# First tokens copied ahead of the first weight split, and a reordered tail, in a one-core encoder layer

## The chip, the core and the metric

One core of a Trainium2 chip. The metric is device time in microseconds of one execution. The engines are TensorE (PE, with PEld for its weight loads), VectorE (DVE), ScalarE (ACT), GpSimd (POOL) and SyncE (SP, which here only issues DMAs and waits). Each runs its own instruction stream in order, and streams meet only at semaphores.

## The reference

Two sequences go through one layer: a sample of 1024 tokens and a prompt of 512, width 1024, float32.

```
h = rmsnorm(x, norm1_g)
proj = h @ w_in                          # q, k, v, z, xBC, dt
x = x + concat(diff_attention(q, k, v), bidirectional_ssd(z, xbc, dt)) @ w_out
h = rmsnorm(x, norm2_g)
aff = softmax(h @ w_router)              # per sequence
gate, idx = top_k(aff.T, cap)            # 16 experts, cap 128 (sample) and 64 (prompt) tokens each
ye = (silu(h[idx] @ w_gate) * (h[idx] @ w_up)) @ w_down * gate
x = x.at[idx].add(ye)
y = rmsnorm(x, final_g)
```

## The kernel before

**Precision and weights.** Every product of two float32 matrices is made of three matmuls of rounded parts: high x high, high x low, low x high. So each weight chunk of 128 x 2048 is loaded (SP), its high part is copied by ACT (`whi`, L780; in the experts L1128) and its low part is a subtraction (`wlo`): by DVE for the first chunk (L1188) and in the experts (L1749), by POOL for the chunks of the input projection (L559). Tokens are treated alike: PE turns (transposes) a normed tile (L1854), ACT copies the high part (`tokens_hi`, L796), DVE makes the low part (`tokens_lo`, L1208).

**Token tiles.** There are 12 tiles of 128 tokens, 0 to 7 of the sample and 8 to 11 of the prompt, in blocks of four: b = 0, 1 (sample) and b = 2 (prompt). A tile is loaded by POOL into one of two slots. `rms(t)` on ACT squares and sums (L786) and takes the root (L789), `normed(t)` on DVE does mean, reciprocal and scaling (L1197 to L1200).

**The opening.** DVE and ACT work out small constants. Then ACT: rms(0), rms(1), split(0); DVE: wait for the gain, normed(0), normed(1), split(0), five small set-up instructions (selectors, L1245 to L1250), and three clears (L1257 to L1259). In the block loop ACT goes tokens_hi(0), rms(2), tokens_hi(1), rms(3), tokens_hi(2), tokens_hi(3), and DVE goes tokens_lo and normed in the same order, then the sin product (L1269). PE turns tiles 0 and 1; then the first 256 token columns of column tile 0 (24 matmuls), tile 2's turn, the first 256 columns of column tile 1, tile 3's turn. It waits for all low parts and starts the steady stretch of 25 column tiles. The first matmuls need the low parts of the first chunk and of tiles 0 and 1. The three clears run at the start of each sequence, so at the prompt's too. There DVE's stretch behind the sin product holds 16 choosing rounds (`choose`, L1215 to L1217) for the sample's top-k and 8 convolution steps (L1317, L1319) beside the rotations (L1276 to L1285). POOL's splits run beside them.

**The experts.** Expert e has 12 chunks: 0 to 7 gate and up, 8 to 11 down. Chunks 8 and 9 make half 0 of the output columns, 10 and 11 half 1. At step j, ACT and DVE split chunk j + 2. Each expert's rows are scattered with an add into `acc_dram`, which holds the residual. The loop is unrolled for the last two, e = 14 (`LATE`) and e = 15.

**The tail.** The final norm needs all experts. Tiles 0 to 3 are loaded (`fin`), squared (L1095), normed (L1675) and stored while expert 14 runs, without the rows of experts 14 and 15. Tiles 4 to 11 follow during expert 15, without its rows. Rows that expert 14 changed are gathered again (`fix_s` 128 of the sample, `fix_p` 64 of the prompt), normed (L1699) and stored over the early ones by POOL (L755, L758). Rows that expert 15 changes are gathered (`xe_s`, `xe_p`), the expert's output is added on the chip half by half (`end_half`: L1720, L1721 for the prompt, L1716 for the sample), normed (L1800) and stored last by POOL (L762, L765). SP holds the stores of tiles 4 to 11 (L493) until both `fix` stores have landed; POOL holds the last two until all tiles are stored. `final_stage` says at which step of expert 14 or 15 the squares, roots and norms run, `norm_order` in which order the squares count.

Of the kernel before, what the change touches and what calls it, by code (L numbers as in the profile page):

```python
# [75 lines left out]
def hybrid_encoder(nc, x, w_in, w_out, w_moe, params, consts, rope, gains, y):  # L76
# [10 lines left out]
    with ctx:  # L87
# [91 lines left out]
        fix_s = at("fix_s", S0 + 16, [P, D])  # L179
# [32 lines left out]
        fi_s = at("fi_s", o + 3.4, [P, 1], U32)  # L212
# [70 lines left out]
        x2_out = [sem(f"x2_out{i}") for i in range(4)]  # L283
        h2_out = [sem(f"h2_out{i}") for i in range(4)]
# [12 lines left out]
        y_in = [sem(f"y_in{i}") for i in range(4)]  # L297
# [56 lines left out]
        def final_tile(t):  # L354

            if t < 11:
                return fin[:, t % 7, :]
# [65 lines left out]
        def _(sp):  # L423
# [58 lines left out]
            def load_final(t):  # L482

                if t == 7:
# [5 lines left out]
            def store_final(t):  # L490

                sp.wait_ge(fy, t + 1)
                sp.dma_start(y[t * P:(t + 1) * P, :], final_tile(t)).then_inc(y_out, 16)  # L493
# [4 lines left out]
            for j in range(ECH):  # L498
                load_moe(LATE, j)
                if j == 5:  # L500

                    sp.wait_ge(scattered, LATE + 1)
                for t in {5: (0, 1), 6: (2,), 7: (3,)}.get(j, ()):
                    load_final(t)
# [11 lines left out]
            for j in (8, 9, 10):  # L516
                chunk_split(sp, last, j)
                for t in ((7, 8), (9,), (10, 11))[j - 8]:
                    load_final(t)

            sp.wait_ge(fix_out, 32)
            for t in range(4, NT):
                store_final(t)
# [3 lines left out]
        def _(pool):  # L527
# [10 lines left out]
            for s, (t0, nt, blocks, cap) in enumerate(SEQS):  # L538
# [126 lines left out]
                for j in range(nt):  # L665
                    t = t0 + j
                    pool.wait_ge(h2_done, t + 1)
                    if t >= 4:
                        pool.wait_ge(x2_out[t % 4], 16 * (t // 4))
                    pool.dma_start(acc_dram[t * P:(t + 1) * P, :], x2[:, j, :]).then_inc(x2_out[t % 4], 16)  # L670
                    pool.dma_start(h2_dram[t * P:(t + 1) * P, :], h2[:, t % 4, :]).then_inc(h2_out[t % 4], 16)
                for i in range(4):
                    pool.wait_ge(x2_out[i], 16 * (t0 + nt) // 4)
                    pool.wait_ge(h2_out[i], 16 * (t0 + nt) // 4)
# [92 lines left out]
            pool.wait_ge(end_out, 32)  # L767
# [3 lines left out]
        def _(act):  # L771
# [58 lines left out]
            rms(1)  # L830
            split(0)
            for s, (t0, nt, blocks, cap) in enumerate(SEQS):
# [4 lines left out]
                for b in blocks:  # L837

                    for j in range(TPB):
                        t = TPB * b + j  # L840
                        if t not in (8, 9):
# [3 lines left out]
                        if j < 2:  # L845
                            rms(t + 2)
# [232 lines left out]
            def final_square(n):  # L1079

                if n < NT:
                    act.wait_ge(y_in[n % 4], 16 * (n // 4 + 1))
                    src, out = final_tile(n), small[:, 0, n:n + 1]
                elif n < 14:
                    act.wait_ge(fix_in, 32)
                    src, out = ((fix_s[:, :], small[:, 4, 0:1]), (fix_p[:, :], small[0:64, 4, 1:2]))[n - 12]
                else:
                    half, i = (0, 0, 1, 1)[n - 14], (0, 1, 1, 0)[n - 14]
# [12 lines left out]
            def final_stage(e, j):  # L1101

                for n in {(LATE, 6): (0,), (LATE, 7): (1,), (LATE, 8): (2, 3), (LATE + 1, 6): (12, 13),
                          (LATE + 1, 7): (4,)}.get((e, j), ()):
# [3 lines left out]
                if (e, j) == (LATE + 1, 8):  # L1108
                    act.wait_ge(fms, 2)
                    act.activation(small[:, 6, 0:1], small[:, 5, 0:1], ACT.Sqrt)  # L1110
                    act.activation(small[0:64, 6, 1:2], small[0:64, 5, 1:2], ACT.Sqrt)
                    roots(2, small[:, 1, 4:5], small[:, 2, 4:5])
                    final_square(5)
                    final_square(6)
                if (e, j) == (LATE + 1, 9):
                    final_square(7)
                    final_square(8)
                    roots(3, small[:, 1, 5:9], small[:, 2, 5:9])

            def expert(e, last, unrolled=True):  # L1120
                act.activation(mark2[0:1, 15:16], mark2[0:1, 0:1], ACT.Silu)
                for j in range(ECH):
# [22 lines left out]
                    if j in (9, 11) and last:  # L1145
# [3 lines left out]
                        if half == 0:  # L1149
                            for n in norm_order[3]:  # L1150
                                final_square(n)
                            roots(4, small[:, 1, 9:NT], small[:, 2, 9:NT])
                        else:
                            final_square(16)
                            roots(5, small[0:64, 5, 5:6], small[0:64, 6, 5:6])
                            final_square(17)
# [24 lines left out]
        def _(dve):  # L1181
# [12 lines left out]
            def normed(t):  # L1194
# [4 lines left out]
                own.link(dve.reciprocal(small[:, 3, t:t + 1], small[:, 2, t:t + 1]))  # L1199
# [1127 lines left out]
```

## Time and profile before

| | us |
|---|---|
| median of 3 runs | 2072.57 (2071.02 to 2072.91) |
| the profiled execution | 2071.08 |
| its span | 2069.3 |
| mean granted clock | 0.957 |
| PE busy | 1890.5 (91%) |
| DVE busy | 1510.1 (73%) |
| ACT busy | 1070.1 (52%) |
| POOL busy | 538.2 (26%) |
| DMA | 329.26 MB, mean 159 GB/s |

Busy time is summed over the instructions of an engine; the span runs from the first to the last instruction. The chain that ended last is followed back from the last instruction to whatever released each step, so it says where a shorter instruction would have mattered. A granted clock of 1.0 is 2.4 GHz for TensorE, 0.5 is 1.2 GHz.

### The profile page before, as it was taken

How to read it: one execution, taken by the hardware profiler on the slowest of the kernel's cores; microseconds unless marked ns; L12 is line 12 of the kernel's file. 1: busy time of each engine (PE TensorE's matmuls, PEld its weight loads, DVE VectorE, ACT ScalarE, POOL GpSimd, SP SyncE). 2: the span in 40 equal slices, each digit the busy share in tenths (PEclk: the TensorE clock that was granted, in tenths of full speed). 3: DMA queues.
4: the chain of work that ended last, by engine and by line, in shares of the span. 5: the costliest groups of instructions: out<-in, count | busy, mean ns of one | idle time of the engine just before them, and what ended most of it. 6: DMA issues, size and time to landing. Idle time of an engine off the chain costs nothing.

```text
span 2069.3 us, 31716 instructions
## 1 busy us (share of the span) xinstructions
PE 1890.5 (91%) x11584; PEld 1682.1 (81%) x11584; DVE 1510.1 (73%) x2226; ACT 1070.1 (52%) x1533; POOL 538.2 (26%) x395
## 2 busy tenths in 40 slices
PE   5998997998889989877884999999999999999995
PEld 5887875787669988655684999999999999999994
DVE  3234784997776659988666787777777778787786
ACT  3233335887572333247632556565555555656574
POOL 2434435330771123352611011111110001111111
PEclk9999998999999989989896999999999999999997
DMA  5233221000023333220134677777777777777886
GB/s 186 98 112 127 88 85 62 1 1 1 16 67 133 143 114 104 77 72 1 41 113 188 219 244 263 253 254 253 239 248 237 250 261 240 267 243 264 294 283 220
DMA packets 62435, 329.26 MB, mean 159 GB/s; under 512 B 7376, under 2 KB 13648, under 8 KB 31760
## 3 DMA queue, kind: packets, MB, share of 16 engines
q1 hardware_dynamic: 46032, 268.63, 36.9%
q0 software_dynamic: 16320, 59.52, 9.8%
q8 instruction: 53, 0.87, 0.2%
q14 instruction: 30, 0.25, 0.0%
HBM read 291.16 MB, written 35.39 MB: 158 GB/s over the span
## 4 chain that ended last, share of the span: by engine, by line
PE 74%; DVE 16%; issue 3%; ACT 3%; DMA 2%; POOL 2%; SPq 0%; DVEq 0%; ACTq 0%; POOLq 0%
PE psum L2209 18%; PE psum L1840 9%; PE psum L1842 9%; PE psum L1841 9%; PE psum L2210 8%; DVE conv_acc L1319 3%; PE psum L2232 2%; PE psum L2231 2%; PE psum L1947 2%; DVE ostat L1400 2%; PE psum L1928 1%; PE psum L2063 1%; DVE prob L1372 1%; PE psum L1929 1%; PE psum L1937 1%
## 5 line engine op out<-in xcount | busy, mean ns | idle before, releaser
L2209 PE MATMUL psum<-xT,whi 128*128 128x384 f32 x1024 | 295.1, 360 | 1.2 <-DVE xT L1815 1.2
L2209 PE MATMUL psum<-xT,whi_x 128*128 128x384 f32 x1024 | 293.7, 359 | 0.0
L1840 PE MATMUL psum<-ht_hi,whi 128*128 128x512 f32 (+1 forms) x648 | 248.9, 384 | 31.5 <-DVE ht_lo L1208 13.5
L1749 DVE TENSOR_TENSOR wlo_x<-wraw_x,whi_x 128x2048 fp32r<-128x2048 f32 x96 | 218.4, 2287 | 57.6 <-ACT whi_x L1128 57.6
L2210 PE MATMUL psum<-xT,wlo 128*128 128x192 f32 x1024 | 257.1, 251 | 0.0
L2210 PE MATMUL psum<-xT,wlo_x 128*128 128x192 f32 x1024 | 256.4, 250 | 0.0
L1841 PE MATMUL psum<-ht_lo,whi 128*128 128x512 f32 (+1 forms) x648 | 246.5, 380 | 0.0
L1842 PE MATMUL psum<-ht_hi,wlo 128*128 128x512 f32 (+1 forms) x648 | 246.4, 380 | 0.0
L559 POOL TENSOR_TENSOR wlo<-wraw,whi 128x2048 fp32r<-128x2048 f32 x39 | 181.4, 4652 | 236.8 <-ACT whi L780 236.8
L1749 DVE TENSOR_TENSOR wlo<-wraw,whi 128x2048 fp32r<-128x2048 f32 x94 | 213.5, 2284 | 16.7 <-ACT whi L1128 16.7
L2210 PEld LDWEIGHTS psum<-xT,wlo 128*128 128x128 f32 x1024 | 196.5, 192 | 0.6
L2210 PEld LDWEIGHTS psum<-xT,wlo_x 128*128 128x128 f32 x1024 | 195.6, 191 | 0.0
L2209 PEld LDWEIGHTS psum<-xT,whi 128*128 128x128 f32 x1024 | 193.3, 189 | 2.2 <-issue 1.6
L2209 PEld LDWEIGHTS psum<-xT,whi_x 128*128 128x128 f32 x1024 | 192.2, 188 | 0.0
L1128 ACT ACTIVATE whi_x<-wraw_x 128x2048 fp32r<-128x2048 f32 x96 | 179.9, 1905 | 3.2 <-DMA wraw_x<-moe_chunks 2.0
L1128 ACT ACTIVATE whi<-wraw 128x2048 fp32r<-128x2048 f32 x94 | 177.8, 1911 | 2.4 <-DMA wraw<-moe_chunks 2.4
L721 POOL TENSOR_TENSOR pmark<-pmark 1x1 f32<-1x1 f32 x15 | 2.7, 183 | 664.1 <-DVE ye_p L1808 664.1
L1840 PEld LDWEIGHTS psum<-ht_hi,whi 128*128 128x128 f32 x648 | 126.0, 194 | 56.5 <-issue 17.8
L1842 PEld LDWEIGHTS psum<-ht_hi,wlo 128*128 128x128 f32 x648 | 125.9, 194 | 22.1
L1841 PEld LDWEIGHTS psum<-ht_lo,whi 128*128 128x128 f32 x648 | 125.9, 194 | 21.4
L780 ACT ACTIVATE whi<-wraw 128x2048 fp32r<-128x2048 f32 x49 | 93.5, 1908 | 63.7 <-PE psum L1842 62.4
L1319 DVE SCALAR_TENSOR_TENSOR conv_acc<-xbc,par,conv_acc 128x1024 f32<-128x1024 f32 (+1 forms) x64 | 124.7, 1949 | 2.3
(367 smaller groups left out, 4349.7 us busy)
## 6 DMA issues: line engine op xcount, KB each, us to landing
wraw<-moe_chunks SPq DMA_DIRECT2D x96, 1024.0 KB, 5.1
wraw_x<-moe_chunks SPq DMA_DIRECT2D x96, 1024.0 KB
wraw<-w_in_chunks SPq DMA_DIRECT2D x39, 1024.0 KB, 5.0
wraw<-w_out_chunks SPq DMA_DIRECT2D x8, 1024.0 KB, 5.6
xin<-x POOLq DMA_DIRECT2D x12, 512.0 KB, 5.2
acc_scratch<-x POOLq DMA_DIRECT2D x12, 512.0 KB, 3.4
h_scratch<-h POOLq DMA_DIRECT2D x12, 512.0 KB, 4.1
fin<-acc_scratch SPq DMA_DIRECT2D x11, 512.0 KB, 9.2
```

Of the source, the lines that this page charges most:

```text
L559: pool.tensor_tensor(wlo[:, g % 2, :, :], wraw[:, g % 2, :].rearrange("p (k n) -> p k n", k=KT), whi[:, g % 2, :, :].bitcast(F32), ALU.sub ...
L780: act.activation(whi[:, g % 2, :, :], wraw[:, g % 2, :].rearrange("p (k n) -> p k n", k=KT), ACT.Copy).then_inc(w_hi_done, 1)
L1128: act.activation(moe_hi[i % 4], moe_raw[i % 4].rearrange("p (k n) -> p k n", k=KT), ACT.Copy).then_inc(w_hi_done, 1)
L1319: ins = stt(out=acc[:, 0:L], in0=xbc[:, i, w:w + L], scalar=p_("conv_w", 5 * i + w), in1=acc[:, 0:L], op0=ALU.mult, op1=ALU.add)
L1400: dve.tensor_reduce(ostat[:, 0, 2 * (u % 2) + c_:2 * (u % 2) + c_ + 1], psum[:, 1024 * c_:1024 * c_ + L], AX.X, ALU.max, negate=True).then ...
L1749: tt(moe_lo[i % 4], moe_raw[i % 4].rearrange("p (k n) -> p k n", k=KT), moe_hi[i % 4].bitcast(F32), ALU.subtract).then_inc(w_lo_done, 1)
L1840: mm(out, wh, xh, start=first, stop=False, **kw)
L1841: mm(out, wh, xl, start=False, stop=False, **kw)
L1842: return mm(out, wl, xh, start=False, stop=final, **kw)
L1947: last = mm(pb[6 + (w // 4) % 2][:, (w % 4) * P:(w % 4 + 1) * P], wgtT[:, w % 2, kk * P:(kk + 1) * P], v[:, kk, h * P:(h + 1) * P], start= ...
L2209: mm(bank[:, 0:2 * TOK], hi[:, k, cols], xT[:, k, :], start=(k == 0), stop=False)
L2210: last = mm(bank[:, 0:TOK], lo[:, k, cols], xT[:, k, 0:TOK], start=False, stop=(k == KT - 1))
```

## The change

In the opening, ACT's order becomes rms(0), rms(1), tokens_hi(0), split(0), tokens_hi(1), rms(2), rms(3), tokens_hi(2), tokens_hi(3). DVE's becomes normed(0), normed(1), tokens_lo(0), split(0), tokens_lo(1), normed(2), normed(3), tokens_lo(2), tokens_lo(3), and then set-up and clears. PE turns tiles 2 and 3 one after the other and computes the first columns of column tile 1 behind both. In the prompt's block the clears move behind the tokens' low parts.

In the tail, tiles are taken in the order 8 to 11, 0 to 7 (`final_rows`). The early four are now the prompt's, so only `fix_p` is left to be corrected and everything of `fix_s` goes. The norm steps that stood at steps 7 and 8 of expert 15 move to step 9, behind the last weight split, and those of tiles 6 to 11 behind it. Six semaphores instead of four count the loads, and loads 7 to 11 are issued together. The last wait moves from POOL to SP. Row stores of `acc` and `h2` share semaphores.

```diff
-        norm_order = ((0, 1, 2, 3), (12, 13, 4), (5, 6, 7, 8), (14, 15, 9, 10, 11), (16, 17))
+        def final_rows(n):
+            t = (n + SEQS[0][1]) % NT
+            return slice(t * P, (t + 1) * P)
+        norm_order = ((0, 1, 2, 3), (12, 4, 5), (6, 7, 8), (9, 10, 11), (13, 14, 15, 16))
...
 # SP
-                if t >= 4:
-                    sp.wait_ge(fss, squared(t - 4))
-                sp.dma_start(final_tile(t), acc_dram[t * P:(t + 1) * P, :]).then_inc(y_in[t % 4], 16)
+                if n >= 6:
+                    sp.wait_ge(fss, squared(n - 6))
+                sp.dma_start(final_tile(n), acc_dram[final_rows(n), :]).then_inc(y_in[n % 6], 16)
-            for j in (8, 9, 10):
-                chunk_split(sp, last, j)
-                for t in ((7, 8), (9,), (10, 11))[j - 8]:
-                    load_final(t)
-            sp.wait_ge(fix_out, 32)
+            chunk_split(sp, last, 8)
+            for n in range(7, NT):
+                load_final(n)
+            sp.wait_ge(fix_out, 16)
...
+            sp.wait_ge(end_out, 32)
 # POOL
-            pool.indirect_dma_start(out=fix_s[:, :], out_offset=None, in_=acc_dram, in_offset=rows_at(si_s)
-                                    ).then_inc(fix_in, 16)
-            pool.indirect_dma_start(out=y, in_=fix_s[:, :], in_offset=None, out_offset=rows_at(fi_s)
-                                    ).then_inc(fix_out, 16)
-            pool.wait_ge(fixed, 2)
-            pool.wait_ge(end_out, 32)
-                        pool.wait_ge(x2_out[t % 4], 16 * (t // 4))
+                        pool.wait_ge(rows_out[t % 4], 32 * (t // 4))
 # ACT
             rms(1)
+            tokens_hi(0)
             split(0)
+            tokens_hi(1)
+            rms(2)
+            rms(3)
-                        if t not in (8, 9):
+                        if t not in (0, 1, 8, 9):
-                        if j < 2:
+                        if b and j < 2:
                             rms(t + 2)
-                for n in {..., (LATE + 1, 6): (12, 13), (LATE + 1, 7): (4,)}
+                for n in {..., (LATE + 1, 6): (12,), (LATE + 1, 7): (4,), (LATE + 1, 8): (5,)}
-                if (e, j) == (LATE + 1, 8):     # roots 2, squares 5, 6; at step 9: squares 7, 8, roots 3
+                if (e, j) == (LATE + 1, 9):     # roots 2, squares 6, 7, 8, roots 3
 # DVE
+                if t == 0:
+                    dve.wait_ge(gain_in, 16)
-            dve.wait_ge(gain_in, 16)
             normed(0)
             normed(1)
+            tokens_lo(0)
             split(0)
+            tokens_lo(1)
+            normed(2)
+            normed(3)
-                dve.memset(tmp[:, :, :], 0.0).then_inc(tmp_clear, 1)
-                own.step(dve.memset(xbc[:, :, 0:2], 0.0))
-                own.link(dve.memset(xbc[:, :, 2 + L:4 + L], 0.0))
...
+                    if b == 0:
+                        selectors()
+                    if b == blocks[0]:
+                        dve.memset(tmp[:, :, :], 0.0).then_inc(tmp_clear, 1)
+                        own.step(dve.memset(xbc[:, :, 0:2], 0.0))
+                        own.link(dve.memset(xbc[:, :, 2 + L:4 + L], 0.0))
 # DVE, expert 15
-                if (e, j) == (LATE + 1, 7):     # means of fix_s, fix_p, 4
-                if (e, j) == (LATE + 1, 8):     # reciprocals; norms of fix_s, fix_p, 4
+                if (e, j) == (LATE + 1, 9):     # means and reciprocals of fix_p, 4, 5; norms of fix_p, 4, 5; means of 6 to 8
...
                         if half == 0:
+                            roots_in(3, 6, 9)
+                            final_norm(6)
+                            end_half(e, 0, 0)
+                            end_half(e, 0, 1)
                             final_norm(7)
+                            dve.wait_ge(fss, squared(11))
+                            mean_squares(9, NT)
                             final_norm(8)
+                            roots_in(4, 9, NT)
+                            for n in range(9, NT):
+                                final_norm(n)
+                            dve.wait_ge(fss, squared(14))
...
                         else:
+                            end_half(e, 1, 1)
+                            end_half(e, 1, 0)
 # PE
-                        if j >= 2:
+                        if j >= 2 and (b or j == 2):
                             column_tile(j - 2, early)
                         if t not in (4, 8, 9):
                             turn_tokens(t)
+                    if b == 0:
+                        column_tile(1, early)
```

## Rows read from the trace of the kernel before

**Rows 1.** The page, part 4: the chain that ended last, by engine.
```profile
PE 74%; DVE 16%; issue 3%; ACT 3%; DMA 2%; POOL 2%; SPq 0%; DVEq 0%; ACTq 0%; POOLq 0%
```
**Rows 2.** PE's waits, 0 to 110: us in total, times, longest us.
```profile
PE psum L1840 <- DVE ht_lo L1208: 10.3, 2, 8.8
```
**Rows 3.** The timeline, 0 to 60: start us, us, instruction [idle before <-releaser].
```profile
13.93 1.91 ACT L780 ACTIVATE whi<-wraw 128x2048 fp32r<-128x2048 f32 x1 [1.31 <-DMA wraw<-w_in_chunks]
...
15.86 1.08 ACT L796 ACTIVATE ht_hi<-psum 128x512 fp32r<-128x512 f32 x2
...
18.08 0.37 DVE L1245 TENSOR_REDUCE head_sel<-cst 128x4 f32<-128x128 f32 x1
...
18.50 1.06 ACT L786 ACTIVATE junk<-xin 128x1024 bf16<-128x1024 f32 x1 [1.55 <-DMA xin<-x]
...
23.50 1.28 DVE L1208 TENSOR_TENSOR ht_lo<-psum,ht_hi 128x512 fp32r<-128x512 f32 x2
...
24.93 0.55 PE L1840 MATMUL psum<-ht_hi,whi 128*128 128x256 f32 x1 [8.77 <-DVE ht_lo L1208]
...
28.26 0.30 PE L1840 MATMUL psum<-ht_hi,whi 128*128 128x256 f32 x1
...
29.35 1.04 PE L1854 MATMUL psum<-cst,xin 128*128 128x128 f32 x8
...
30.14 0.36 PE L1840 MATMUL psum<-ht_hi,whi 128*128 128x256 f32 x1
...
33.09 1.03 PE L1854 MATMUL psum<-cst,xin 128*128 128x128 f32 x8
...
35.70 0.39 PE L1840 MATMUL psum<-ht_hi,whi 128*128 128x256 f32 x1 [1.58 <-DVE ht_lo L1208]
```
**Rows 4.** Windows: stretch, length, busy PE, PEld, DVE, ACT, POOL; clock, DMA share, GB/s.
```profile
750.00:755.30 5.30, 5.27 (x25) 5.30 (x26) 3.52 (x9) 3.72 (x7) 1.08 (x2) 0.50 0.30 99
...
2036.20:2042.20 6.00, 6.00 (x14) 4.74 (x15) 5.66 (x7) 2.40 (x7) 0.70 (x1) 0.50 0.68 257
...
2042.00:2043.00 1.00, 1.00 (x6) 0.83 (x5) 1.00 (x2) 0.96 (x1) 0.00 (x0) 0.92 1.02 418
```
**Rows 5.** The timeline of DVE in the prompt's opening, 749 to 807.
```profile
749.98 0.91 DVE L1257 MEMSET tmp<- 128x1024 f32 x1 [0.20 <-issue]
...
761.54 0.48 DVE L1269 TENSOR_SCALAR sin_t<-sin_t,lamt 128x512 f32<-128x512 f32 x1
...
782.05 3.95 DVE L1317 TENSOR_SCALAR conv_acc<-xbc,par 128x512 f32<-128x512 f32 x1
...
806.54 2.10 DVE L1285 TENSOR_TENSOR qT<-stage,cos_t 128x512 f32<-128x512 f32 x1 [1.99 <-ACT stage L864]
```
**Rows 6.** The timeline of POOL there.
```profile
762.67 4.62 POOL L559 TENSOR_TENSOR wlo<-wraw,whi 128x2048 fp32r<-128x2048 f32 x1 [11.25 <-ACT whi L780]
```
**Rows 7.** The timeline of ACT in the tail: chunk 10's split.
```profile
2025.80 1.90 ACT L1128 ACTIVATE whi_x<-wraw_x 128x2048 fp32r<-128x2048 f32 x1
```
**Rows 8.** The timeline of DVE in the tail.
```profile
2033.84 2.28 DVE L1749 TENSOR_TENSOR wlo_x<-wraw_x,whi_x 128x2048 fp32r<-128x2048 f32 x1
...
2039.08 0.74 DVE L1716 SCALAR_TENSOR_TENSOR xe_s<-psum,gcur_s,xe_s 128x512 f32<-128x512 f32 x1
...
2041.12 2.46 DVE L1675 SCALAR_TENSOR_TENSOR fin<-fin,small,gain 128x1024 f32<-128x1024 f32 x2
...
2046.47 2.48 DVE L1675 SCALAR_TENSOR_TENSOR fin<-fin,small,gain 128x1024 f32<-128x1024 f32 x2
...
2050.07 0.68 DVE L1720 TENSOR_TENSOR ye_p<-psum,tp 64x512 f32<-64x512 f32 x1
```
**Rows 9.** The timeline of PE in the tail: the start of half 1.
```profile
2036.17 0.79 PE L2231 MATMUL psum<-whi_x,hid 128*128 128x512 f32 x1 [2.91 <-DVE wlo_x L1749]
```
**Rows 10.** The timeline of SP in the tail: the first stores of the last eight.
```profile
2040.04 1.58 SPq L493 DMA_DIRECT2D y<-fin  x3
```
**Rows 11.** The timeline of POOL in the tail: the store before the last.
```profile
2054.97 1.82 POOL L762 DMA_INDIRECT y<-xe_p,gi_p  x1 [18.07 <-DVE xe_p L1800]
```

More of the change, by code:

```diff
@@ L282, in hybrid_encoder @@
                                                             sem("h2_turned"), sem("h2T_out"))
-        x2_out = [sem(f"x2_out{i}") for i in range(4)]
-        h2_out = [sem(f"h2_out{i}") for i in range(4)]
+        rows_out = [sem(f"rows_out{i}") for i in range(4)]
         lg_done = sem("lg_done")
@@ L296, in hybrid_encoder @@
         sc_s, sc_p = sem("sc_s"), sem("sc_p")
-        y_in = [sem(f"y_in{i}") for i in range(4)]
+        y_in = [sem(f"y_in{i}") for i in range(6)]
         fss, fms, frms, fy, y_out = sem("fss"), sem("fms"), sem("frms"), sem("fy"), sem("y_out")
@@ L515, in _ @@
                     load_final(j - 1)
[L516 to L523 removed]
+            chunk_split(sp, last, 8)
+            for n in range(7, NT):
+                load_final(n)
+            sp.wait_ge(fix_out, 16)
+            for n in range(4, NT):
+                store_final(n)
+            sp.wait_ge(end_out, 32)
         @block.gpsimd
@@ L1107, in final_stage @@
                     roots(1, small[:, 1, 0:4], small[:, 2, 0:4])
-                if (e, j) == (LATE + 1, 8):
+                if (e, j) == (LATE + 1, 9):
                     act.wait_ge(fms, 2)
-                    act.activation(small[:, 6, 0:1], small[:, 5, 0:1], ACT.Sqrt)
                     act.activation(small[0:64, 6, 1:2], small[0:64, 5, 1:2], ACT.Sqrt)
[L1112 to L1118, printed above, removed]
+                    roots(2, small[:, 1, 4:6], small[:, 2, 4:6])
+                    for n in (6, 7, 8):
+                        final_square(n)
+                    roots(3, small[:, 1, 6:9], small[:, 2, 6:9])
             def expert(e, last, unrolled=True):
@@ L1149, in expert @@
                         if half == 0:
-                            for n in norm_order[3]:
+                            for n in (9, 10, 11):
                                 final_square(n)
                             roots(4, small[:, 1, 9:NT], small[:, 2, 9:NT])
-                        else:
+                            final_square(13)
+                            final_square(14)
+                        else:
+                            final_square(15)
+                            roots(5, small[0:64, 5, 5:6], small[0:64, 6, 5:6])
                             final_square(16)
-                            roots(5, small[0:64, 5, 5:6], small[0:64, 6, 5:6])
-                            final_square(17)
                             roots(6, small[:, 5, 3:4], small[:, 6, 3:4])
@@ L1262, in _ @@
                         t = TPB * b + j
-                        if t not in (8, 9):
+                        if t not in (0, 1, 8, 9):
                             tokens_lo(t)
-                        if j < 2:
+                        if b and j < 2:
                             normed(t + 2)
+                    if b == 0:
[4 more added lines that the diff above has]
+                        own.link(dve.memset(xbc[:, :, 2 + L:4 + L], 0.0))
                     tok = block_tile(b) * P
@@ L1687, in final_stage @@
                         final_norm(t)
-                if (e, j) == (LATE + 1, 7):
-                    dve.wait_ge(fss, squared(4))
-                    ts(small[:, 5, 0:1], small[:, 4, 0:1], 1.0 / D, EPS, ALU.mult, ALU.add)
+                if (e, j) == (LATE + 1, 9):
+                    dve.wait_ge(fss, squared(5))
                     ts(small[0:64, 5, 1:2], small[0:64, 4, 1:2], 1.0 / D, EPS, ALU.mult, ALU.add)
-                    mean_squares(4, 5)
-                if (e, j) == (LATE + 1, 8):
+                    mean_squares(4, 6)
                     dve.wait_ge(frms, 2)
-                    own.step(dve.reciprocal(small[:, 7, 0:1], small[:, 6, 0:1]))
                     own.step(dve.reciprocal(small[0:64, 7, 1:2], small[0:64, 6, 1:2]))
-                    roots_in(2, 4, 5)
-                    for rows, a, col in ((P, fix_s, 0), (64, fix_p, 1)):
-                        stt(out=a[:, :], in0=a[:, :], scalar=small[0:rows, 7, col:col + 1],
-                            in1=gain[0:rows, :], op0=ALU.mult, op1=ALU.mult).then_inc(fixed, 1)
+                    roots_in(2, 4, 6)
+                    stt(out=fix_p[:, :], in0=fix_p[:, :], scalar=small[0:64, 7, 1:2],
+                        in1=gain[0:64, :], op0=ALU.mult, op1=ALU.mult).then_inc(fixed, 1)
                     final_norm(4)
-                if (e, j) == (LATE + 1, 9):
+                    final_norm(5)
                     dve.wait_ge(fss, squared(8))
-                    mean_squares(5, 9)
-                    roots_in(3, 5, 9)
-                    final_norm(5)
-                    final_norm(6)
+                    mean_squares(6, 9)
             def end_half(e, half, i):
```

69 lines of the change are left out of this document (30 added, 39 removed).

## The prediction

> **What bounds the kernel now.** I read the page first: TensorE (PE) is three quarters of the chain that ended last, so time is to be had only where PE stands idle or where the chain leaves it [rows 1]. PE's waits in the opening come next: two waits of 10.3 us together for the tokens' low parts on VectorE (DVE), one of them 8.8 [rows 2]. The timeline of the opening shows why: PE starts its first columns at 24.93 and its steady stretch at 35.70, and from 18.08 to 23.50 DVE is in set-up, tile 0's low part and the norm of tile 2; only then comes tile 1's low part, on which PE waits [rows 3]. In the prompt's opening DVE has slack early and none later [rows 5]. In the tail PE waits 2.91 us for the low half of the last weight chunk [rows 9] and then runs at granted clock 0.50, its 1.2 GHz level, for six microseconds [rows 4]; yet the kernel ends on DVE: last norms, last sums, last two stores [rows 8, 11].
>
> **The head, part by part** [rows 3].
> 1. Added ahead of the first split: the two copies of tile 0 on ScalarE (ACT), 1.08 us. ACT had waited for the weights until 13.93, and PE began to turn tile 0 at about 12.5, so the first copy fits into that wait and the second ends near 14.5. The split, DVE's half of it and all behind them move by +0.55.
> 2. Removed between DVE's half of the split and tile 1's low part: 23.50 - 18.08 = 5.42 (tile 0's low part now runs while DVE waits for the split). PE's first columns start at 24.93 - 5.42 + 0.55 = 20.1, which is 4.9 earlier. They keep their length to the turn of tile 2, 29.35 - 24.93 = 4.4.
> 3. PE's order behind them. Before: turn of tile 2 at 29.35, columns of tile pair 1 at 30.14, turn of tile 3 at 33.09, then 1.58 of waiting for its copies, 35.70: 6.35 in all. Now the two turns stand together (0.8 each) and the columns (33.09 - 30.14 = 2.95) run while tile 3 is copied, which took 35.70 - 33.09 = 2.6: 4.5 in all, no wait. Saved 1.8.
> 4. Tile 2 has landed at 18.50, where ACT's square of it starts; its norm is over by 22 and PE asks for it at 24.5. Tile 3's landing can't be seen, since its square stood behind DVE; PE asks at 25.3. Both cost nothing unless tile 3 comes over 2 us later than tile 2 did; beyond that, a microsecond for each.
> 5. Set-up and clears now run behind tile 3's low part, where DVE has nothing to do until the ninth column tile: 0. The wait for the gain moves behind a reciprocal: 0, as the weights and not the norm hold the split. ACT's next weight split still follows tile 3's copies and moves with them.
> Sum of the head: 4.9 + 1.8 = 6.7. Bounds: in PE's first 24 matmuls the row at 28.26 is the first at 0.12 apart, sixteen before it stood at 0.21. All 24 slow adds 0.8, none slow saves 1.5: 5.9 to 8.2.
> The granted clock was 0.50 all through the same columns in the prompt's opening [rows 4], so the bounds are both reached somewhere. The Trainium skill (TensorE: Matmul & The Clock Gate, "What's actually happening") says that how many matmuls run at the lower level after a rest varies from run to run; the two openings agree with it. By it the sum would be the same, with those bounds.
>
> **The middle** [rows 5, 6]. In the prompt's stage the clears (0.91 and two of 0.07) leave 749.98, where ACT's square and table load were the longer way, and stand ahead of the sin product at 761.54. DVE is then 1.0 late. Its first convolution step already met the end of POOL's second split, the next was held by POOL for 3.95 (the sin product, of the same shape, takes 0.48), and at 806.54 DVE waited 1.99 for ACT: the 1.0 is swallowed at each of these. Value 0; the bad case is rival B. The row stores of acc and h2 now share a semaphore: the h2 store, issued second, was what was waited for anyway. 0.
>
> **The tail** [rows 7 to 9].
> 1. Removed on ACT between its splits of chunks 10 and 11: a table load, roots, and one of two squares. Split 10 stays at 2025.80, one square being ahead of it in both; then 1.9, one square of 1.06 and 1.9 for split 11, which ends at 2030.7.
> 2. Removed on DVE ahead of its half of chunk 11: three norms and their reciprocals. That half starts at 2030.7 instead of 2033.84 and ends at 2032.9. PE's 2.91 of waiting go, just, and so do the six microseconds at 0.50; PE ends near 2042.3 instead of 2048.3. That counts for nothing by itself, as DVE is later.
> 3. DVE from 2032.9: a round trip to ACT with reciprocals 0.9; nine norms at 1.20 (2046.47 to 2050.07 is three), the prompt rows of expert 14 and tiles 4 to 11, 10.8; a second round trip 0.7; the three sums of half 0, 2.04 (2039.08 to 2041.12); small steps 0.5. Sum 14.9: the last sums start at 2047.8 instead of 2050.07. From there to the end the sequence is as before. Saved 2.3.
> 4. One gather and one store of 0.5 MB fewer on the queues: 0, nothing on the path waits for them. The final wait passes from POOL to SP: -0.3 to +0.3, by the gaps of 0.2 to 0.3 before an issue; taken 0.
> Bounds: the store gate (rival A) can take 1.5, and the last wait gives 0.3 at most: 0.8 to 2.6.
>
> **Sum.** 6.7 + 0 + 2.3 = 9.0 us. The profiled execution took 2071.08 with a span of 2069.3; it stands 1.5 under the median of 2072.57. So 2062.1 as that execution, and 2063.6 as a median, which I predict. The parts' bounds together are 6.7 to 10.8, or 2061.8 to 2065.9; with 1 us of scatter the forecast's own range is 2061 to 2067.
>
> **Rivals** (times as medians).
> A. The store gate. SP holds the last eight stores until the prompt rows of expert 14 are stored. Before, their norm ended at 2032.6 (one norm ahead of 2033.84) and the first store went at 2040.04 [rows 8, 10]: 7.4 later, with another store's descriptors between. Now the norm ends at 2035.1. With the whole 7.4 the first store goes at 2042.5, without the other's descriptors (some 3) at 2039.6. Eight stores of 0.52 MB at 418 GB/s [rows 4] take 10.0 and start 0.9 late: through at 2050.5 or 2053.4. POOL's next to last store would be ready at 2054.97 - 2.3 = 2052.7 [rows 11]. For: three stores left at once at 2040.04, so this wait was real. Against: an emptier queue. Price 0 to 1.8 with the landing: 2065.4.
> B. The clears meet POOL. The sin product moves behind them, from 761.54 to 762.55, and POOL's split starts at 762.67 [rows 6], 0.12 later. If POOL is first, DVE stands until 767.3; its next steps fall into POOL's splits elsewhere, the last choosing round ahead of the rotations ends at 815.6 instead of 804.6 by the same durations, and after the slack in front of the rotations 5.2 are left, where DVE holds the chain. For: the 3.95, and 2.10 at 806.54. Against: by the rows DVE is first. 2068.8. The Trainium skill (SBUF — State Buffer, "Who interferes with whom") says that whoever issues first keeps the port pair for the whole instruction and the other is fully blocked. The two long rows agree; the price is made of rows alone.
> C. Slower. The same place at its full price: 1.0 for the clears, 4.6 for the first block, 3.7 more at the second and 2.9 more at the rotation, less 1.99 of slack, is 10.2 lost against 9.0 gained: 2073.8. It decides once DVE is over 9.0 late at the second rotation. Against: each block has to hit, and the rotations' transfers absorb nothing.
> D. The head gives half. Weights or tile 3 land late under the same queues, PE starts near 23.5: 3.4 less, 2067.
>
> **Chances.** Forecast 0.63, A 0.12, B 0.16, C 0.03, D 0.06. A measurement of this kernel tells about 0.2% (4.1 us) from no change, so faster means under 2068.4: the forecast, A, D and just under half of B, and 0.01 off for scatter, 0.87. Same is the rest of B and little else, 0.09; slower is C and what I don't see, 0.04. The range reaches into B: 2060.8 to 2069.0.
>
> **What would show it.** PE's first columns near 20.1, its steady stretch near 29.0 and no wait between; DVE's set-up behind tile 3's low part; in the prompt's stage the sin product in under 0.6 us, ahead of POOL; PE's last half without a wait and without a granted 0.50; the last sums at 2050.07 - 9.0 = 2041.1. Wrong would be: a sin product of over 4 us (B), last stores that start more than 0.8 after their norms (A), a first column start after 22 (D), or any stage between the opening and the tail that changes its length by over 1 us.

## The result: 11.4 and 11.9 us faster by the medians, where 9.0 were predicted

| | median us | executions | ratio to before, 95% interval |
|---|---|---|---|
| before | 2072.6 | 2071.0 to 2072.9 | |
| changed | 2061.2 | 2058.7 to 2061.7 | 0.9940, 0.9926 to 0.9955 |
| changed, timed again (e5) | 2060.7 | 2060.0 to 2062.0 | 0.9944, 0.9930 to 0.9958 |

The ratio of 0.9940 is 12.4 us, with an interval from 9.3 to 15.3. The profiled execution took 2060.84 with a span of 2059.0 (before 2071.08 and 2069.3). In the profile after, the opening first: the timeline of PE and of POOL (start us, us, instruction, idle before and its releaser).

```profile
19.86 0.55 PE L1846 MATMUL psum<-ht_hi,whi 128*128 128x256 f32 x1 [4.34 <-DVE ht_lo L1207]
...
24.87 1.91 PE L1860 MATMUL psum<-cst,xin 128*128 128x128 f32 x16
26.54 0.36 PE L1846 MATMUL psum<-ht_hi,whi 128*128 128x256 f32 x1
...
37.93 4.62 POOL L561 TENSOR_TENSOR wlo<-wraw,whi 128x2048 fp32r<-128x2048 f32 x1 [3.87 <-ACT whi L775]
```

The first columns start 5.07 earlier than in [rows 3], both turns stand together, and PE has no further wait. Its waits from 0 to 110 are now these two (us in total, times, longest), the second where [rows 2] had 10.3:

```profile
PE psum L1860 <- DVE xin L1199: 11.8, 1, 11.8
PE psum L1846 <- DVE ht_lo L1207: 4.3, 1, 4.3
```

The set-up, now behind the tokens' low parts, runs into POOL's first split, which begins at 29.45; the prediction did not foresee that. A cast of the selectors, on DVE, takes 4.59 instead of the 0.17 of before (the timeline of DVE):

```profile
29.50 4.59 DVE L1255 CAST unit_row<-conv_acc 128x16 fp32r<-128x16 f32 x1
```

PE doesn't wait for it, as the two waits above show.

The prompt's opening, the timeline of DVE and of POOL. The sin product is 4.79 long where it was 0.48 [rows 5], with POOL's split begun 0.11 ahead of it; in before POOL began 1.13 behind it [rows 6]:

```profile
755.37 4.61 POOL L561 TENSOR_TENSOR wlo<-wraw,whi 128x2048 fp32r<-128x2048 f32 x1 [11.37 <-ACT whi L775]
755.48 4.79 DVE L1278 TENSOR_SCALAR sin_t<-sin_t,lamt 128x512 f32<-128x512 f32 x1
...
799.24 2.10 DVE L1294 TENSOR_TENSOR qT<-stage,cos_t 128x512 f32<-128x512 f32 x1 [0.36 <-ACT stage L863]
```

In the tail, the timeline of ACT, DVE and SP. ACT waits 4.38 for chunk 8 to land; DVE's half of chunk 11 now has no norm ahead of it [rows 8]; the last sums start at 2042.66, 7.41 earlier than in [rows 8]; SP's stores start 5.71 earlier than in [rows 10].

```profile
2009.74 1.92 ACT L1123 ACTIVATE whi<-wraw 128x2048 fp32r<-128x2048 f32 x1 [4.38 <-DMA wraw<-moe_chunks]
...
2022.82 2.29 DVE L1750 TENSOR_TENSOR wlo_x<-wraw_x,whi_x 128x2048 fp32r<-128x2048 f32 x1 [2.34 <-ACT whi_x L1123]
2025.66 2.29 DVE L1750 TENSOR_TENSOR wlo_x<-wraw_x,whi_x 128x2048 fp32r<-128x2048 f32 x1 [0.56 <-ACT whi_x L1123]
...
2034.33 7.34 SPq L495 DMA_DIRECT2D y<-fin  x7
...
2042.66 0.68 DVE L1722 TENSOR_TENSOR ye_p<-psum,tp 64x512 f32<-64x512 f32 x1
```

PE's row of the tail, and the window behind it (length, busy PE, PEld, DVE, ACT, POOL; granted clock, DMA share, GB/s): its wait has not gone, it has moved from the last chunk [rows 9] to chunk 8, and the stretch at 0.50 (the 1.2 GHz level) has moved with it [rows 4].

```profile
2019.12 0.76 PE L1846 MATMUL psum<-whi,hid 128*128 128x512 f32 x1 [3.27 <-DVE ur L1756]
```
```profile
2018.70:2024.70 6.00, 5.58 (x13) 4.45 (x14) 3.50 (x8) 5.39 (x8) 0.00 (x0) 0.50 0.76 292
```

Last, POOL's rows that cut the kernel in three, and the header with the span:

```profile
core 0 of [0], span 2059.0 us
...
1982.85 0.18 POOL L722 TENSOR_TENSOR pmark<-pmark 1x1 f32<-1x1 f32 x1 [40.85 <-DVE ye_p L1814]
...
2047.60 1.81 POOL L758 DMA_INDIRECT y<-xe_p,gi_p  x1 [15.61 <-DVE xe_p L1806]
2049.71 0.97 POOL L761 DMA_INDIRECT y<-xe_s,gi_s  x1 [0.30 <-issue]
```

The same in before:

```profile
core 0 of [0], span 2069.3 us
...
44.24 4.62 POOL L559 TENSOR_TENSOR wlo<-wraw,whi 128x2048 fp32r<-128x2048 f32 x1 [2.93 <-ACT whi L780]
...
1990.08 0.18 POOL L721 TENSOR_TENSOR pmark<-pmark 1x1 f32<-1x1 f32 x1 [40.85 <-DVE ye_p L1808]
...
2057.10 0.97 POOL L765 DMA_INDIRECT y<-xe_s,gi_s  x1 [0.30 <-issue]
```

That last store lands 3.5 us after its issue (the view of the DMAs, before, 2040 to 2075; the last number is us to landing):

```profile
y<-xe_s,gi_s POOLq DMA_INDIRECT x1, 3.5
```

I call three stretches by these rows. **Opening**: up to POOL's second low half (44.24). **Tail**: from POOL's small add ahead of its last scatter, expert 14's (1990.08) to the start of its last store (2057.10). **End**: from there to the span's end. In these two profiles the opening gave 6.3, the tail 67.02 - 66.86 = 0.2, the end 12.2 - 9.3 = 2.9. The middle, between opening and tail, was 0.9 shorter; what that means the experiments show.

### The profile page after: what moved, and what is told of

The parts are those of the page before. It is cut to its first block and busy times, and to the rows that moved or that the text cites. A ratio compares the mean times of both kernels' runs of the same rounds, so it can differ in the third digit from the quotient of the medians.

```text
span 2059.0 us, 31700 instructions
## 1 busy us (share of the span) xinstructions
PE 1891.4 (92%) x11584; PEld 1682.8 (82%) x11584; DVE 1513.7 (74%) x2222; ACT 1067.6 (52%) x1530; POOL 537.9 (26%) x393
```

## The experiments

All stretches below are read from the same rows in each profile.

| kernel | median us | ratio, 95% interval | opening | middle | tail | end |
|---|---|---|---|---|---|---|
| before | 2072.6 | | 44.24 | 1945.8 | 67.0 | 12.2 |
| changed | 2061.2 | 0.9940, 0.9926-0.9955 | 37.93 | 1944.9 | 66.9 | 9.3 |
| e1 before, last wait on SP | 2070.6 | 0.9990, 0.9981-0.9999 | 44.92 | 1946.6 | 67.7 | 9.5 |
| e2 changed, last wait on POOL | 2062.8 | 0.9955, 0.9942-0.9967 | 38.57 | 1945.6 | 64.3 | 12.1 |
| e3 opening alone | 2065.8 | 0.9971, 0.9959-0.9982 | 38.72 | 1945.5 | 67.7 | 12.2 |
| e4 all but the opening | 2067.5 | 0.9972, 0.9962-0.9981 | 44.70 | 1950.1 | 64.3 | 9.3 |
| e5 changed again | 2060.7 | 0.9944, 0.9930-0.9958 | 37.55 | 1947.7 | 64.3 | 9.3 |
| e6 set-up early | 2062.9 | 0.9961, 0.9947-0.9974 | 41.12 | 1945.6 | 64.6 | 9.3 |
| e7 PE's old order | 2064.3 | 0.9961, 0.9947-0.9975 | 39.59 | 1948.6 | 64.3 | 9.4 |
| e8 prompt's clears early | 2059.1 | 0.9937, 0.9924-0.9951 | 37.44 | 1946.2 | 64.4 | 9.4 |
| e9 last wait on ACT | 2061.3 | 0.9939, 0.9925-0.9952 | 37.78 | 1948.1 | 64.3 | 9.3 |
| e10 POOL busy at the end | 2061.4 | 0.9943, 0.9930-0.9957 | 36.69 | 1948.1 | 64.3 | 11.1 |
| e11 early norm | 2058.7 | 0.9930, 0.9917-0.9944 | 37.11 | 1944.7 | 63.0 | 9.4 |
| e12 two early norms | 2056.9 | 0.9921, 0.9907-0.9934 | 38.98 | 1945.7 | 61.1 | 9.3 |

Read the columns first. The middle runs from 1944.7 to 1950.1 without regard to what was changed: most of the scatter of an execution, several us, lies there. Tail and end repeat within 0.7 us, with one exception, and tell parts of a microsecond; a median doesn't.

**e1, the last wait alone.**
```diff
             for t in range(4, NT):
                 store_final(t)
+            sp.wait_ge(end_out, 32)
...
-            pool.wait_ge(end_out, 32)
```


> The kernel before, with one edit: the last wait of the program, for both rows' stores (end_out, 32), is taken from GpSimd's queue and put at the end of SyncE's. Theory W (which queue holds the last wait sets what lies behind the last issue: 12.2 us with GpSimd, 9.3 us with SyncE in the two traces): 2.9 us faster than before, about 2069.7 against 2072.6, and from the last issue to the span's end about 9.3 us; nothing earlier moves. Rival S (the 2.9 us came with the shorter stores ahead of it in the changed kernel, and the prediction's own value of 0 with 0.3 to each side holds for the wait): 2072.3 to 2072.9, and still about 12.2 us behind the last issue.


Measured: end 9.5, tail and opening as before, 2.0 faster in the medians (the interval gives 0.2 to 3.9). The view of POOL:

```profile
core 0 of [0], span 2068.8 us
...
2059.26 0.97 POOL L766 DMA_INDIRECT y<-xe_s,gi_s  x1 [0.30 <-issue]
```

68.8 - 59.26 = 9.5 where before has 69.3 - 57.10 = 12.2. The span itself fell by 0.5 only: this execution was 2.2 late when it got there, 0.7 of it from the opening, 0.8 from the middle and 0.7 from the tail. One span beside another would have hidden the effect. Theory W holds, S falls.

**e2, the changed kernel without that edit.**
```diff
-            sp.wait_ge(end_out, 32)
...
+            pool.wait_ge(end_out, 32)
```


> The changed kernel with the last wait put back on GpSimd's queue and taken from SyncE's. Theory W: 2.9 us slower than the changed kernel, so 8.5 us faster than before, about 2064.1; some 12.2 us between the last issue and the span's end. Rival S: as the changed kernel, about 2061.2, with 9.3 us there.


Measured: end 12.1, so 2.8 longer, as W says; by the medians only 1.6 slower than the changed kernel's first timing and 2.1 than its second, which their scatter doesn't tell from 2.8. Its tail was 64.3, not 66.9: the first sign that the changed kernel's first profile was no typical one.

```profile
core 0 of [0], span 2060.6 us
...
2048.53 0.97 POOL L760 DMA_INDIRECT y<-xe_s,gi_s  x1 [0.30 <-issue]
```

**e3, the opening alone.** The diff's opening parts on ACT, DVE and PE (with the gain wait and the clears), nothing else.


> The kernel before with the opening of the changed one alone (order of tokens, splits, set-up and norms on ScalarE and VectorE, the gain wait, and TensorE's columns of tile 1 behind all turns; the tail, the stores and the last wait are as before). Theory H (the landmarks of the two traces stand 7.3 us apart from the opening to 1990 us, and nothing of it is lost in the tail of before): 7.3 us faster, about 2065.3. The prediction's size for the head: 6.7 us, 2065.9. Rival L (a start 7.3 us earlier meets the memory traffic of the tail otherwise, and part is lost there): 4 to 6 us faster, 2067 to 2069, with the splits of the last expert's chunks 6 to 8 less than 7.3 us ahead of before's.


Measured: 6.8 faster by the medians, 6.0 by the ratio (3.7 to 8.5); tail 67.7 and end 12.2 as before. The opening is 5.9 earlier than the mean of the three with the old one (44.6). The 7.3 that I had read as a constant shift between the first two traces was 6.7 until 300 us and partly the middle's scatter. Nothing is lost in the tail: L falls. 6.7 and 7.3 aren't told apart by this run; all executions with the new opening together do it (below).

**e4, all but the opening.**


> The kernel before with everything of the change but the opening (tile order, load and store order, the tail on ScalarE and VectorE, both waits of the row stores joined, the last wait on SyncE). Theory N (the tail to the last sums gives 0.1 us, since chunks 6 to 8 of the last expert land up to 4.9 us late, and the last wait gives 2.9): 3.0 us faster, 2069.6, the last sums at 2050.0. Rival P (the prediction's tail: the chunks land as before, the last sums are 2.3 us earlier at 2047.8, and the wait's 2.9 comes on top): 5.2 us faster, 2067.4, with TensorE's wait of 3.3 us ahead of chunk 8 gone. By the prediction as it stood (2.3 and 0): 2070.3.


Measured: 5.1 faster by the medians, 5.8 by the ratio (3.9 to 7.9). Tail 64.3, so 2.7 to 3.4 shorter than the three old ones, end 9.3, and no wait of 3.3 ahead of chunk 8 (0.7). P holds, N falls. e3 and e4 together make 11.8 by the ratios, which is the whole.

**e5, the changed kernel again**, no edit.


> The changed kernel as it is, once more. In its first profile the chunks 6 to 8 of the last expert landed up to 4.9 us late, and from GpSimd's last small add ahead of the last scatter (1982.85) to its last store (2049.71) it took 66.9 us; with the same tail that stretch took 64.3 in the two last variants (2049.71's counterpart 2048.53 and 2059.09), and 67.0 to 67.7 with the tail of before. Theory V (the late landing is a matter of the single execution): 64 to 65 us in this profile, TensorE without a wait of over 1 us there and no granted 0.50. Rival F (it belongs to the changed kernel as a whole): 66.5 to 67 again. Time 2060 to 2062 by either.


Measured: tail 64.3. The window of the stretch that stood at 0.50:

```profile
2018.70:2024.70 6.00, 5.73 (x25) 4.78 (x26) 3.49 (x8) 5.53 (x8) 0.00 (x0) 1.00 1.02 410
```

Full clock, and 25 matmuls where the first profile has 13 (the window is the same in time; in the work e5 stands 2.4 later, by its small add at 1985.23). All eight further profiles with this tail (e2, e4 to e10) lie between 64.3 and 64.6, so V holds: the late landing of chunks 6 to 8, PE's wait and the half clock belong to one execution of nine and cost it 2.5. What made those transfers late stays open: the two loads into wraw (chunks 8 and 9) landed 16.3 us after their issue in median, in e5 13.3, in e9 11.9, in e6 13.8. The DMA engines' share was 1.0 in the first profile, in e5 and in e9.

It is the far end of a smaller scatter. PE's wait ahead of chunk 8 in before, e1 and e5 (us in total, times, longest; 2000 to 2050):

```profile
PE psum L1840 <- DVE ur L1755: 0.8, 1, 0.8
```
```profile
PE psum L1840 <- DVE ur L1755: 1.5, 1, 1.5
```
```profile
PE psum L1846 <- issue: 0.7, 1, 0.7
```

e3 has 1.5 too; of the nine with the new tail seven have 0.7, e6 has 1.0 and the first profile 3.3. Take this wait off each tail, and the three old ones are all 66.2 and the nine new ones all 63.6, to 0.1. So the new order of the work gives 2.6, and the rest of any difference between two tails is this wait.

**e6, the set-up back ahead of tile 1's low part.**
```diff
             tokens_lo(0)
             split(0)
+            selectors()
+            dve.memset(tmp[:, :, :], 0.0).then_inc(tmp_clear, 1)
+            own.step(dve.memset(xbc[:, :, 0:2], 0.0))
+            own.link(dve.memset(xbc[:, :, 2 + SEQS[0][1] * P:4 + SEQS[0][1] * P], 0.0))
             tokens_lo(1)
...
-                    if b == 0:
-                        selectors()
-                    if b == blocks[0]:
+                    if s and b == blocks[0]:
```


> The changed kernel with VectorE's set-up (the selectors and the three clears of the first sequence) back where it stood, behind its half of the first weight split and ahead of tile 1's low part; the tokens' order stays. Theory H (the set-up's 2.4 us there, 18.08 to 20.48 in the trace of before, are on the path, and with them TensorE's first columns move from 19.86 to 22.3): 2.4 us slower than the changed kernel, 8.7 to 9.2 us faster than before, about 2063.5. Rival O (only the order of the tokens matters, the set-up falls beside TensorE's work): as the changed kernel, 2061.


Measured: 2.2 slower than e5. The timeline of PE: first columns 2.56 after e5's 19.96.

```profile
22.52 0.55 PE L1848 MATMUL psum<-ht_hi,whi 128*128 128x256 f32 x1 [6.76 <-DVE ht_lo L1207]
```

H holds: of the 5.42 of step 2 the set-up is somewhat under half, the norm of tile 2 and tile 0's low part are the rest.

**e7, PE's order of before.**
```diff
-                        if j >= 2 and (b or j == 2):
+                        if j >= 2:
...
-                    if b == 0:
-                        column_tile(1, early)
```


> The changed kernel with TensorE's order of before in the first block: the columns of tile pair 1 between the turns of tiles 2 and 3, instead of behind them. Theory H (step 3 of the prediction, 1.8 us): TensorE waits 1.5 to 2.0 us for tile 3's copies again, its steady stretch starts that much later, and the kernel is 1.8 us slower than the changed one, about 2063. Rival O (the copies of tile 3 are ready anyway, now that they need no set-up ahead): within 0.5 us of the changed kernel.


Measured: first columns at 20.01, as in e5, then the old wait again:

```profile
31.05 0.39 PE L1846 MATMUL psum<-ht_hi,whi 128*128 128x256 f32 x1 [1.57 <-DVE ht_lo L1207]
```

Its opening is 39.59, 1.7 behind the mean of the nine with the new one (37.9). Those nine run from 36.7 to 39.0, so one execution against their mean proves little. Closer is a comparison with e5 and e9, in which nearly as many of the first 24 columns ran slow (16 and 18, in e7 17): from the first columns to the steady stretch they took 9.15 and 9.39, e7 11.04, so 1.65 to 1.89 more. The median is 3.6 above e5's, but its middle was 0.9 longer and the intervals overlap. H holds.

**e8, the prompt's clears ahead of its tokens.**
```diff
                 if s:
                     phase(dve, ph, phase_dve)
+                    dve.memset(tmp[:, :, :], 0.0).then_inc(tmp_clear, 1)
...
-                    if b == blocks[0]:
+                    if b == blocks[0] and s == 0:
```


> The changed kernel with the three clears of the second sequence (the prompt) back ahead of its tokens; in the first sequence they stay behind them. In the changed kernel's trace the sin product stands 4.79 us behind a split on GpSimd that started 0.11 us before it. Theory A (that stall is swallowed by waits that follow): the product takes under 0.6 us again, and the time is that of the changed kernel, within 0.5 us; the step at GpSimd's landmark near 807 and the last add near 1983 stand 0 apart, relative to the stage's start. Rival B at the prediction's price: 5.2 us faster than the changed kernel, about 2056.


Measured: 1.6 under e5, intervals overlapping. Opening, tail and end don't differ, and the profile decides: POOL's split begins at 755.36, within 0.01 of the changed kernel's 755.37, so the two traces can be laid on each other from there.

```profile
754.22 0.48 DVE L1281 TENSOR_SCALAR sin_t<-sin_t,lamt 128x512 f32<-128x512 f32 x1
...
774.73 3.95 DVE L1329 TENSOR_SCALAR conv_acc<-xbc,par 128x512 f32<-128x512 f32 x1
...
799.22 2.10 DVE L1297 TENSOR_TENSOR qT<-stage,cos_t 128x512 f32<-128x512 f32 x1 [1.98 <-ACT stage L863]
```

The sin product is ahead of POOL and short, a later step is held for 3.95 instead, and the first rotation stands at 799.22 against 799.24. By POOL's rows the two stay within 0.07 up to 1095, ahead of the experts. The stall is real and costs 0.02 at the rotation. A holds; B's price is refuted.

**e9, the last wait on ACT** (`act.wait_ge(end_out, 32)` behind its last expert, SP's taken away).


> The changed kernel with the last wait (end_out, 32) on ScalarE's queue instead of SyncE's. From the start of GpSimd's last store to the span's end the profiles show 12.1 to 12.2 us where GpSimd holds this wait (three profiles) and 9.3 to 9.5 where SyncE does (seven). Theory G (GpSimd takes longer than other engines from its last instruction to the end of the program): 9.3 to 9.5 us here too, 2060 to 2061. Rival Y (SyncE is the special one): 12.1 us, 2.8 us slower than the changed kernel, about 2063.7.


**e10, POOL busy behind its last store.**
```diff
                                     ).then_inc(end_out, 16)
+            pool.memset(ye_p[:, :], 0.0)
+            pool.memset(ye_s[:, :], 0.0)
```


> The changed kernel, and behind GpSimd's last store two memsets of dead tiles on GpSimd (0.95 us each, by a memset of 64x1024 in the trace); the last wait stays on SyncE. Theory G1 (the span ends a fixed 8.4 us behind the end of GpSimd's last instruction, which starts 0.97 earlier and gives the 9.3; where GpSimd holds the wait, the same stretch starts with the landing, 3.55 behind the issue, and gives 12.0): 9.3 + 1.9 = 11.2 us from the last store's start to the span's end, 1.9 us slower than the changed kernel. Rival G2 (with the wait on SyncE the end is set by SyncE: 3.5 to the landing and 5.8 behind it): 9.3 us, the time as the changed kernel's. Between them: GpSimd ends up to some slack ahead of SyncE, and part of the 1.9 shows.


Measured, e9 and then e10, the timeline of POOL:

```profile
core 0 of [0], span 2059.5 us
...
2050.16 0.97 POOL L760 DMA_INDIRECT y<-xe_s,gi_s  x1 [0.30 <-issue]
```
```profile
core 0 of [0], span 2060.2 us
...
2049.06 0.97 POOL L761 DMA_INDIRECT y<-xe_s,gi_s  x1 [0.30 <-issue]
...
2050.92 0.96 POOL L764 MEMSET ye_s<- 128x1024 f32 x1
```

ACT as holder gives 9.3, as SP does: Y falls. And with 1.9 of work behind the store the end grows by 1.8, to 11.1: the span ends 8.3 behind POOL's last instruction (2051.88 to 2060.2), as it does in the changed kernel (2050.68 to 2059.0). G1 holds, G2 falls. The median of e10 is only 0.7 above e5's, which the times can't resolve; the profile can.

**e11 and e12, less on DVE at the end.** These follow from step 3: DVE had 14.7 of work behind the last half (2027.81 to 2042.52 in e5), and 2.35 idle ahead of chunk 10's. The core of the edit (e12 adds tile 4 in the same way):
```diff
                     if j == 7 and last:
+                        act.wait_ge(fixm, 1)
+                        act.activation(small[0:64, 6, 1:2], small[0:64, 5, 1:2], ACT.Sqrt).then_inc(fixr, 1)
...
+                if (e, j) == (LATE + 1, 7):
+                    dve.wait_ge(fixr, 1)
+                    own.link(dve.reciprocal(small[0:64, 7, 1:2], small[0:64, 6, 1:2]))
+                    stt(out=fix_p[:, :], in0=fix_p[:, :], scalar=small[0:64, 7, 1:2],
+                        in1=gain[0:64, :], op0=ALU.mult, op1=ALU.mult).then_inc(fixed, 1)
```


> The changed kernel with the norm of the prompt rows of expert 14 moved from behind VectorE's half of chunk 11 into its idle 2.35 us ahead of its half of chunk 10; its root on ScalarE stands in the 3.28 us in which ScalarE waits for hm; and the squares of tiles 6 and 7 ahead of the roots of 4 and 5. Theory D (VectorE alone holds the end from the last weight half on, 14.8 us of work): 1.3 us of norm and 0.4 us of steps less, the last sums 1.7 us earlier counted from GpSimd's add ahead of the last scatter, so 62.6 us from it to the last store instead of 64.3, and about 2059. Rival P (the extra work delays chunk 10 by as much on ScalarE or VectorE, or the stores' gate is next): 64 us, 2060.5 or more.

> As the variant before, and the norm of tile 4 too: its square on ScalarE ahead of the copies of hm, its root behind them, its norm on VectorE behind that of the prompt rows, ahead of the half of chunk 10 (which starts some 0.3 us later by it). Theory D: 2.9 us fewer on VectorE behind the last half; with TensorE's end and ScalarE's copy of its last bank at 39.5 on the changed kernel's scale, where the last sums then start at 39.6, the gain is just reached: 61.4 to 61.7 us from GpSimd's add to the last store, about 2058. Rival P (the weight halves of chunks 10 and 11 come late and TensorE becomes the end): 62.5 to 64 us, no better than the variant before, and a wait for wlo_x on TensorE.


Measured: tails of 63.0 and 61.1, so 1.3 and 3.2 shorter than 64.3 (D said 1.7, and 2.6 to 2.9: 0.4 too much and 0.3 too little), and PE without a wait of over 0.7 in both. The rows of DVE in e12: both norms stand in the gap, and both halves run as one stretch.

```profile
2019.92 1.28 DVE L1706 SCALAR_TENSOR_TENSOR fix_p<-fix_p,small,gain 64x1024 f32<-64x1024 f32 x1
...
2021.30 1.28 DVE L1690 SCALAR_TENSOR_TENSOR fin<-fin,small,gain 128x1024 f32<-128x1024 f32 x1
2022.51 4.49 DVE L1759 TENSOR_TENSOR wlo_x<-wraw_x,whi_x 128x2048 fp32r<-128x2048 f32 x2
...
2038.74 0.68 DVE L1729 TENSOR_TENSOR ye_p<-psum,tp 64x512 f32<-64x512 f32 x1
```

D holds in kind in both, P falls. e12 is the fastest of all: 2056.9, ratio 0.9921 against the changed kernel's 0.9940 and 0.9944. Its interval overlaps theirs; the tail shows the difference, the times alone wouldn't.

## What of the prediction held, and the term that failed

The likeliest case came, its steps of head and tail in their places, with one of the signs that the prediction had named as wrong (rival B's, at no cost). But the sum was 2.4 to 2.9 us short by the medians. The median of 2061.2 lies at the lower edge of the stated range of 2060.8 to 2069.0; by the ratio, 0.9940 of 2072.6, it would be 2060.2, below that range, and the ratio's interval leaves the 9.0 out. By the stretches: 6.8 + 3.1 + 2.8 = 12.7 against 9.0; the times show 11.4 to 11.9, the rest being scatter.

**Head, 6.7 predicted.** The nine profiles with the whole new opening average 37.9 for it, before, e1 and e4 44.6: 6.8. Step 2 said first columns at 20.1: in the nine they start between 19.01 and 20.42, at 19.8 in the mean. Step 3 said 1.8 (e7: 1.7). In the first profile the steady stretch began near 29.5 instead of 29.0, because 21 of the first 24 matmuls stood at 0.21 apart; in before it was 15 (the prediction counts 16), and in the fourteen profiles 13 to 24. The Trainium skill says of this count that it varies from run to run (TensorE: Matmul & The Clock Gate, "What's actually happening"), and these profiles agree; the bounds had it. Step 5's 0 held too, though the set-up met POOL's split and its cast took 4.59: PE had no wait from it.

**Middle, 0 predicted.** Nothing speaks against it in sum. But the middle varies by 5.4 among the profiles, so it can't show a change of 1 us, which the prediction had named as a sign of being wrong; only e8's rows can. One part was wrong: the clears did put the sin product behind POOL, by 0.11, which the prediction held for the less likely order by 0.12. The clears, priced at 1.0, took 1.26 (the product starts at 754.22 in e8, at 755.48 in the changed kernel), which is more than that margin; in all ten profiles with the clears there the product takes 4.78 or 4.79. The Trainium skill's rule (SBUF — State Buffer, "Who interferes with whom": the first to issue keeps the port pair for its whole instruction) agrees with 755.37 ahead of 755.48, and with the cast at 29.50 behind POOL's 29.45. But rival B's price of 5.2 was added up from stalls without taking away those of before that vanish: a DVE that is late by 4.3 meets the later splits elsewhere, and the 3.95 of [rows 5] is gone in the changed kernel. e8 measures the exchange: 0.02.

**Tail, 2.3 predicted.** With chunks 6 to 8 on time it is 67.0 to 67.7 before and 64.3 after: 2.7 against before's own profile, 3.1 against the mean of three. Step 3's 14.9 of work on DVE were 14.7, and that work began 0.2 earlier than step 2 had it (42.6 behind the small add in e5, 42.8 predicted). With these two 0.2 the 2.3 become 2.7. Against the mean it is 3.1, because the wait ahead of chunk 8 was 0.8 to 1.5 with the old tail and 0.7 to 1.0 in eight of nine with the new. Whether the gather and the store that fell away (step 4's other 0) shortened it isn't shown. The first profile of the changed kernel hid nearly all of the 2.7, by a late transfer that no step of mine foresaw and whose cause stays open. The last sums came at 2042.66 there, not at 2041.1.

**The failing step is tail step 4**: "The final wait passes from POOL to SP: -0.3 to +0.3, by the gaps of 0.2 to 0.3 before an issue; taken 0." I priced the wait by what an issue costs, and never asked what lies behind it. The profile of before had the row: its last store starts at 2057.10 and lands 3.5 later, at 2060.6, and the span ends at 2069.3. Those 8.7 us behind the last transfer were in plain sight and on no list of mine; the term was taken 0 and measured 2.8. POOL takes 8.3 to 8.7 from its last instruction or wait to the end of the program, and the kernel before started that only with the landing; with the wait elsewhere it starts at once and runs beside the transfer, whose landing (3.5) and what follows on the other engine fit inside. e1, e2, e9 and e10 show this from four sides. It was worth 2.8, three quarters of the 3.7 that the stretches have over my sum. What the engine does in those 8 us no row shows.

**Rivals.** A did not come: the stores started 4.35 behind the end of the prompt rows' norm (2029.98), which is A's 7.4 without the other store's 3, the cheap end of its price, and POOL's store at 2047.60 was released by DVE's norm. B came as an event (a product of 4.79, over the 4 that the prediction had named) and cost nothing; C, the same place at a higher price, fell with B's price. D did not come.

## What to carry to other kernels

Look at what lies behind the last instruction as at any other stretch: from the last store's start to the span's end, engine by engine, and let no engine with a long way to its end hold the wait for the last transfer. Price a stall that moves by the difference of both traces, the vanished ones too, not by the sum of the new ones. Compare stretches between named rows over several profiles before you explain a shift of one or two microseconds between two.

## What the runs showed of the hardware

- The span ends 8.3 us behind GpSimd's last instruction when another engine holds the last wait (changed kernel, e9 and e10), and 8.5 to 8.7 behind the landing when GpSimd does (before, e2 and e3). What GpSimd does in that time no row shows. SyncE and ScalarE as holders are alike: 9.3 to 9.5 from the last store's start in ten profiles without work behind it.
- In one of nine profiles with the new tail two weight chunks landed 16.3 us after their issue in median (11.9 in e9, 13.3 in e5, 13.8 in e6), with the DMA engines' share at 1.0 there as in e5 and e9; TensorE then stood for 3.27 us and ran the next six at a granted clock of 0.50. The cost was 2.5 us.
- One stall of VectorE behind GpSimd's split (4.79 for a product that takes 0.48) and another, later one (3.95) in its place left the next rotation within 0.02 us. A cast of 0.17 took 4.59 behind another split (29.50), and TensorE waited for nothing.
- Of the first 24 matmuls behind the opening's wait, 13 to 24 ran at 0.21 us apart and the rest at 0.12, in fourteen profiles.
